# Query products from the third block of weights on in 16 bit parts

## What is computed

```python
def peer(h, peer_w_query, peer_keys1, peer_keys2, peer_u, peer_v):
    ...
    def block(xb):
        qh = (xb @ peer_w_query).reshape(-1, PEER_HEADS, 2, PEER_KEY_DIM // 2).astype(jnp.float32)
        s1 = jnp.einsum('thd,kd->thk', qh[:, :, 0], peer_keys1.astype(jnp.float32))
        s2 = jnp.einsum('thd,kd->thk', qh[:, :, 1], peer_keys2.astype(jnp.float32))
        v1, i1 = lax.top_k(s1, PEER_TOPK)
        v2, i2 = lax.top_k(s2, PEER_TOPK)
        ...
        act = jax.nn.gelu(jnp.einsum('thkd,td->thk', peer_u[e], xb).astype(jnp.float32))
        return jnp.einsum('thk,thkd->td', (g * act).astype(xb.dtype), peer_v[e])
```

## Time and profile before

| | us |
|---|---|
| median of three runs | 5007.54 |
| lowest and highest of the three | 4987.62, 5008.25 |
| profiled execution, device time | 5001.89 |
| its span in the trace | 5000.0 |
| TensorE busy with matmuls | 4677.6 (94% of the span) |
| VectorE busy | 2859.6 (57%) |
| ScalarE busy | 1316.0 (26%) |
| query phase on TensorE, first to last product | 2023.2 to 2292.4 |

### The profile page before, as it was taken

The page is one execution under the profiler, slowest core; times in us unless marked ns, Lnnn a source line. Parts: engine busy times, 40 slices in busy tenths (PEclk is TensorE's granted clock), DMA queues, the critical chain, the costliest instruction groups (busy, mean ns, idle before and its releaser), DMA issues. The chain is left out here.

```text
span 5000.0 us, 70223 instructions
## 1 busy us (share of the span) xinstructions
PE 4677.6 (94%) x26702; PEld 2940.9 (59%) x26702; DVE 2859.6 (57%) x5220; ACT 1316.0 (26%) x1829; POOL 782.6 (16%) x743
## 2 busy tenths in 40 slices
PE   5999989999778799899999999999997999999996
PEld 4666644555676465566666666666664555555553
DVE  3456414433355434314666766667543989889884
ACT  2223213332110000211444444444222222222221
POOL 0000100000000001000000000000002766666640
PEclk6999987876676899899999999999998999999998
DMA  4443532211233344223455555545445888888861
GB/s 152 163 160 122 175 103 64 69 56 54 83 107 105 136 170 176 75 68 130 169 194 191 180 190 184 205 176 189 168 155 211 311 301 294 292 297 300 293 231 72
DMA packets 367537, 846.13 MB, mean 169 GB/s; under 512 B 35986, under 2 KB 198418, under 8 KB 358482
## 3 DMA queue, kind: packets, MB, share of 16 engines
q1 hardware_dynamic: 251122, 472.45, 27.7%
q0 software_dynamic: 72352, 272.81, 15.7%
q10 hardware_dynamic: 43840, 97.93, 5.2%
HBM read 665.05 MB, written 178.03 MB: 169 GB/s over the span
## 5 line engine op out<-in xcount | busy, mean ns | idle before, releaser
L364 PE MATMUL dot_ps<-h_parts,u_parts 128*128 128x384 f16 (+1 forms) x9216 | 1452.9, 317 | 7.2 <-PEq L1846 4.5
L364 PEld LDWEIGHTS dot_ps<-h_parts,u_parts 128*128 128x128 f16 x9216 | 892.5, 98 | 498.3 <-issue 6.5
L364 PE MATMUL totals_ps<-act_parts,v_parts 128*128 128x416 f16 x6144 | 1083.8, 340 | 33.3 <-DVE act_parts L2728 33.2
L364 PEld LDWEIGHTS totals_ps<-act_parts,v_parts 128*128 128x128 f16 x6144 | 601.5, 98 | 514.3 <-issue 36.4
L377 PE MATMUL in_ps<-h_parts_in,in_parts 128*128 128x384 f16 (+1 forms) x3168 | 492.3, 318 | 5.3 <-DVE in_parts L693 4.5
L2443 DVE SCALAR_TENSOR_TENSOR u_parts<-u_chunks,units,u_parts 128x1024 f16<-128x1024 f32 x126 | 161.8, 1284 | 516.4 <-ACT u_parts L2227 516.4
L2236 ACT ACTIVATE gelu<-dot_ps,units 128x384 f32<-128x384 f32 (+1 forms) x384 | 215.9, 563 | 808.0 <-PE dot_ps L364 807.9
L377 PEld LDWEIGHTS in_ps<-h_parts_in,in_parts 128*128 128x128 f16 x3168 | 309.2, 98 | 182.5 <-DVE in_parts L693 4.6
L2795 POOL DMA_INDIRECT row_value<-tmp_g_rows,row_g x256 | 307.6, 1202 | 394.1 <-POOLq L2101 316.2
L2684 ACT ACTIVATE v_parts<-v_group,units 128x1024 f16<-128x1024 f32 x128 | 136.6, 1137 | 768.0 <-PE totals_ps L364 712.9
L2739 DVE SCALAR_TENSOR_TENSOR h<-totals_ps,sum_unit,h 128x416 f32<-128x416 f32 x388 | 247.6, 647 | 140.7 <-PE totals_ps L364 137.2
(11 more groups left out here) (340 smaller groups left out, 5598.8 us busy)
## 6 DMA issues: line engine op xcount, KB each, us to landing
u_chunks<-in_u SPq DMA_DIRECT2D x128, 512.0 KB, 5.6
v_sweep<-in_v SPq DMA_DIRECT2D x128, 512.0 KB, 4.7
v_group<-in_v SPq DMA_DIRECT2D x32, 2048.0 KB
tmp_g<-gelu ACTq DMA_DIRECT2D x128, 416.0 KB, 2.7
tmp_w<-h POOLq DMA_DIRECT2D x26, 2048.0 KB, 8.4
w_groups<-tmp_w SPq DMA_DIRECT2D x32, 1664.0 KB
gelu_in<-tmp_g SPq DMA_DIRECT2D x32, 1664.0 KB
merge_sweep<-in_u POOLq DMA_DIRECT2D x64, 512.0 KB, 5.5
```

The lines of the kernel that those rows point to most:

```text
L364: mm = pe.matmul(bank, left(x), right(y), start=first and x == 0 and y == 0, stop=last and x == 1)
```

## The change

Three things change.

1. From block 2 on (`WIDE = 2`) queries(c) is done in 16 bit parts, with `triple`: 72 float16 products in place of 24 float32 ones. For this each block of `w_query` is split too, into `wq16`, two buffers: the leading part by ScalarE (`lead_part`), the rest by VectorE (`rest_part`). Blocks 0 and 1 stay in float32.
2. The tokens' parts `h16` are made at once, all eight chunks behind `scales.ready` and ahead of queries(2), which now waits for them. For this `spread_out` moves up behind the first third of queries(1). The parts of the first two chunks of `u` move behind the takes of blocks 2 and 3.
3. The scale of `w_query` needs its largest value. The merge sweeps its sixteen blocks too: five sweeps in place of four to an output chunk, 80 in place of 64, with a ring of five buffers. Two further operations write `W_SCALE` and `Q_UNIT`, and one further reduction takes the largest of the sixteen.

At the start of the phase the loads of `wq` are now issued ahead of the load of the keys.

```diff
-        sweep = Sweep(nc, ctx, sem, "merge", a, s, SWEPT, NK - SWEPT, 4, [])
+        EACH = 5
+        sweep = Sweep(nc, ctx, sem, "merge", a, s, SWEPT, NK - SWEPT, EACH, [], 2 * EACH, range(2 * EH))
...
-                        for k in range(4):
-                            sweep.vector(dve, i, 4 * u + k)
+                        for k in range(EACH):
+                            sweep.vector(dve, i, EACH * u + k)
...
             def _(sp):
-                sp.dma_start(keys[:, :, :], a["keys"]).then_inc(keys_in, 16)
                 for c in range(RQ):
                     sp.dma_start(wq[:, c, :, :], a["w_query"][c]).then_inc(wq_in[c], 16)
+                sp.dma_start(keys[:, :, :], a["keys"]).then_inc(keys_in, 16)
...
-                        sp.wait_ge(q_done, (c + 1) * NS)
+                        if c < WIDE:
+                            sp.wait_ge(q_done, (c + 1) * NS)
+                        else:
+                            sp.wait_ge(wq_split, c - WIDE + 1)
...
-                def queries(c):
-                    pe.wait_ge(wq_in[c % RQ], 16 * (c // RQ + 1))
+                def queries(c, beside=None):
+                    if c < WIDE:
+                        pe.wait_ge(wq_in[c], 16)
+                    else:
+                        pe.wait_ge(h_split, KC)
+                        pe.wait_ge(wq_split, c - WIDE + 1)
...
+                            else:
+                                mm = triple(pe, q_ps[:, at % 4, 0:n], lambda x: wq16[:, c % 2, x, k, :],
+                                            lambda y: h16[:, y, k, t0:t0 + n], k == 0, k == KC - 1)
                         mm.then_inc(q_done, 1)
+                        if beside and q == 0:
+                            beside()
...
-                queries(1)
-                scales.spread_out(pe, 0)
+                queries(1, lambda: scales.spread_out(pe, 0))
...
+                def lead_part(c):
+
+                    act.wait_ge(wq_in[c % RQ], 16 * (c // RQ + 1))
+                    if c >= WIDE + 2:
+                        act.wait_ge(q_done, (c - 1) * NS)
+                    act.activation(wq16[:, c % 2, 0, :, :], wq[:, c % RQ, :, :], ACT.Copy,
+                                   scale=units[:, W_SCALE:W_SCALE + 1]).then_inc(wq_hi, 1)
...
-                for c in range(3):
+                take(0)
+                act.wait_ge(scales.ready, 1)
+                for k in range(KC):
+                    act.activation(h16[:, 0, k, :], h[:, k, :], ACT.Copy, scale=h_unit[:, 1:2]).then_inc(h_hi, 1)
+                lead_part(WIDE)
+                take(1)
+                lead_part(WIDE + 1)
+                for c in range(WIDE, K2):
                     take(c)
...
+                    if c + 2 < K2:
+                        lead_part(c + 2)
...
+                def rest_part(c):
+                    dve.wait_ge(wq_hi, c - WIDE + 1)
+                    dve.scalar_tensor_tensor(wq16[:, c % 2, 1, :, :], wq[:, c % RQ, :, :],
+                                             units[:, W_SCALE:W_SCALE + 1], wq16[:, c % 2, 0, :, :], ALU.mult,
+                                             ALU.subtract).then_inc(wq_split, 1)
+
+                for k in range(KC):
+                    dve.wait_ge(h_hi, k + 1)
+                    dve.scalar_tensor_tensor(h16[:, 1, k, :], h[:, k, :], h_unit[:, 1:2], h16[:, 0, k, :],
+                                             ALU.mult, ALU.subtract).then_inc(h_split, 1)
+                rest_part(WIDE)
+                take(0)
+                rest_part(WIDE + 1)
+                for c in range(1, K2):
...
+                    if WIDE + 2 <= c + 3 < K2:
+                        rest_part(c + 3)
```

More of the change, by code:

```diff
@@ L170, in build @@
             gain=keep("gain", [P, KC, 1 + NSEQ]),
-            u_tops=keep("u_tops", [P, NK]),
+            u_tops=keep("u_tops", [P, NK + 2 * EH]),
             units=keep("units", [P, 8]),
@@ L280, with __init__ @@
     STEP = 8
-    def __init__(self, nc, ctx, sem, name, a, s, first, count, ring, spare):
+    def __init__(self, nc, ctx, sem, name, a, s, first, count, ring, spare, step=STEP, also=()):
         self.a, self.s, self.first, self.count, self.ring = a, s, first, count, ring
+        self.step, self.also = step, also
         fresh = ring - len(spare)
-        own = ctx.enter_context(nc.sbuf_tensor(name + "_sweep", [P, fresh, KC * P], F32))
+        own = ctx.enter_context(nc.sbuf_tensor(name + "_sweep", [P, fresh, KC * P], F32)) if fresh else None
         self.buf = spare + [own[:, r, :] for r in range(fresh)]
@@ L1810, in _ @@
                                   spare[:, u, :, :]).then_inc(mix_taken, 1)
-                        for k in range(4):
-                            sweep.vector(dve, i + KC // 2, 4 * u + k)
+                        for k in range(EACH):
+                            sweep.vector(dve, i + KC // 2, EACH * u + k)
                 norm.vector(dve)
@@ L1824, in sb @@
             return ctx.enter_context(nc.sbuf_tensor(name, shape, dt))
-        K2, NT, RQ = 2 * EH, TILES + 1, 4
+        K2, NT, RQ, WIDE = 2 * EH, TILES + 1, 4, 2
         keys = sb("keys", [P, 2, NK])
         wq = sb("wq", [P, RQ, KC, P])
+        wq16 = sb("wq_parts", [P, 2, 2, KC, P], F16)
         qh = sb("qh", [P, 2, TP])
@@ L1909, in take @@
                         act.wait_ge(q_done, at + 1)
+                        unit = units[:, Q_UNIT:Q_UNIT + 1] if c >= WIDE else 1.0
                         if q == NS - 1:
-                            act.copy(qh[:, c % 2, T:TP], q_ps[:, at % 4, SEQ - t0:n]).then_inc(twice, 1)
-                        act.copy(qh[:, c % 2, t0:t0 + n], q_ps[:, at % 4, 0:n]).then_inc(q_taken, 1)
-                act.sem_inc(q_taken, 4)
-                for c in range(3):
-                    take(c)
-                act.wait_ge(scales.ready, 1)
@@ L1918, in _ @@
-                for c in range(2):
-                    act.wait_ge(s["u_in"][c], 16)
-                    act.activation(u16[:, 0, c, :, :], u[:, c, :, :], ACT.Copy,
-                                   scale=units[:, U_SCALE:U_SCALE + 1]).then_inc(s["u_hi"], 1)
-                for c in range(3, K2):
-                    if c < 3 + KC:
-                        k = c - 3
-                        act.activation(h16[:, 0, k, :], h[:, k, :], ACT.Copy,
-                                       scale=h_unit[:, 1:2]).then_inc(h_hi, 1)
-                    take(c)
+                            act.activation(qh[:, c % 2, T:TP], q_ps[:, at % 4, SEQ - t0:n], ACT.Copy,
+                                           scale=unit).then_inc(twice, 1)
```

51 lines of the change are left out of this document (28 added, 23 removed).

## The result

The changed kernel is faster: 4964.31 us in the median of six runs against 4997.2 in six of the kernel before. The ratio is 0.9916 with a 95% interval from 0.9892 to 0.9939, that is 42 us less, with 30 to 54 inside the interval; it is not the ratio of the two medians, which lie 33 us apart. One run of the changed kernel took 12098.69 us, more than twice any other; it is left out of the ratio, and its cause is open. The forecast was 46.6 us less, 4958 us.

The account below looks back on a forecast made before the run. The prediction took TensorE to bound the merge and query phase. It summed −48.6 (16 bit products) + 2.4 (wait) − 0.4 (load order) = −46.6 us, giving 4958 us, range 4938 to 4980.

Parts of the forecast that it names:

- Bound by TensorE: Merge and query phase: TensorE is the bound, busy 158.22 of 160 and 180.00 of 180 us; other engines have room.
- The 16 bit products: Query blocks from 2 on: 14.63 to 11.16 us each, 3.47 less, over fourteen blocks 48.6 us less.
- The wait ahead of queries(2): Before queries(2): TensorE stalls 2.4 us for the chain from spread_out through VectorE's eight rests and block 2's rest.
- The clock after the stall: Behind the wait before queries(2): a possible half-speed loss of 1.6 us, left out of the sum.
- the rival: Behind the wait before queries(2): the clock falls, one loss of 1.6 us, total 4960 us; chance 0.28.
- Splits, sweeps, loads: Query phase and merge: splits and sixteen further sweeps stay hidden, adding nothing; issuing the wq load first saves 0.4 us.
- All phases behind the queries as long as before: Dots phase and later: a sign of the forecast, no change in their lengths.
- a rival in which the gain is given back later: Dots phase start: set by something other than TensorE, such as the last scores' store; about 5000 us, chance 0.04.
- The level of 4958 us: Whole kernel: 4958 us, chosen with sums of 4955.3 from the profiled execution and 4960.9 from the runs' median.

Follow-up runs that it names:

- e2: Changed kernel with spread_out moved back behind queries(1): query phase 238.1 us against 226.1, ratio to the kernel before 0.9933.
- e4: Changed kernel with block 2's weights split before the tokens and queries(2) waiting chunk by chunk: query phase 223.5 us, ratio to before 0.9879.
- e7: Changed kernel executed once more without an edit, for its trace: query phase 226.7 us, dots phase 1561.9 us.
- e9: Changed kernel plus 20 unused float32 products (40 matmul instructions) ahead of the merge's branch loop: dots phase 1552.2 us, ratio to before 0.9909.
- e5: Changed kernel with every sweep of the merge done twice: merge 389.7 us, query phase 227.6 us, ratio to before 0.9924.
- e1: Kernel before with only the change's sixteen further sweeps and five buffers, queries left float32: merge 390.6 us, ratio to before 0.9989.
- e3: Changed kernel with 16 bit parts only from block 8 on: query phase 245.0 us, dots phase 1555.0 us, ratio to before 0.9962.
- e8: Kernel before executed once more without an edit, for its trace: query phase 273.4 us, dots phase 1551.8 us.
- e12: Kernel before plus 20 unused float32 products (40 matmul instructions) in the merge: query phase 273.3 us, dots phase 1551.9 us.

## Why the prediction was right, and where it was not

**Bound by TensorE.** Right. Both stages stayed without a gap, and a faster block moved the end by just what it saved.

**The 16 bit products.** Right, and a little short: 3.57 us a block instead of 3.47, 50.0 us in all. I took 11.16 us from the earlier trace rows, where the small matmul of the spread, which ends the stretch, starts 0.1 us late. Behind it in the same trace 216 such matmuls in one piece start at 208.39 and are followed at 241.58, which is 11.06 us for 72.

**The wait ahead of queries(2).** Right: 2.44 us against 2.4, by the steps that were named. The late spread (e2) and the waits by chunk (e4) show that this chain sets it.

**The clock after the stall.** The loss was left out of the sum, and in the trace of after it did not come: 19 matmuls ran in the first 3.0 us, at clock 1.00. That was in part luck. Of the four traces with this wait of 2.28 us, three (after, e7, e9) kept the clock, and e5 lost 1.68 us behind it. Behind 11.74 us (e2) the clock was at 0.50. So the reason given, that 2.4 us is nearer to the short gap, does not decide it: the rival happens in some executions.

**Splits, sweeps, loads.** Right: no wait in the steady state, a merge as long as before in e1 and with twice the sweeps in e5. The first product starts 0.48 us earlier behind its idle time (27.85 instead of 28.33 us; 0.4 was forecast). The other traces agree: 28.4 to 29.2 us with the keys first, 27.9 to 28.1 with the weights first. That the merge came out at 391.4 us both times in spite of it is chance: its first products lost 1.8 us more to the clock after the change, and those of the norm 1.7 us less.

The query phase is thus accounted for: −49.98 us for the blocks, +2.44 for the wait, −0.46 because the clock rose earlier in queries(0) (17.00 to 16.54 us), +0.35 in the idle time ahead of the dots phase (4.49 to 4.84 us), together −47.65, and −47.64 is measured. That idle time stands in this row:

```profile
2251.65 68.61 PE L365 MATMUL dot_ps<-h_parts,u_parts 128*128 128x384 f16 x426 [4.84 <-PEq L1850]
```

**All phases behind the queries as long as before.** This step failed. The dots phase took 8.4 us more, and 7.8 to 9.7 more in the two traces of the kernel as against its twin with 40 further matmuls (e9: 1552.2). I had a rival in which the gain is given back later, but for another reason, a start of the dots phase that does not follow TensorE, and with all of the gain. What came in its place is the changed length of TensorE's program: the second idle time at each jump, 5.5 us in the trace of after, and the lower clock behind one of them; the transfers of instructions (last section) show what TensorE waits for there. By the stages the gain is 47.6 less 8.4, that is 39 us. The whole came out at 42 and not at 47, which fits, but an interval of 30 to 54 can't tell 39 from 47.

**The level of 4958 us.** It was hit within 7 us, and that is in part luck. It was taken between two sums, and the higher of them rests on 5007.54 us, the median of three runs of before; the median of six is 4997.2. Less 46.6 that would be 4950.6, and 4964.31 is 13.7 above it.

## What to carry to other kernels

Where one engine is busy without a gap, price an edit by the start-to-start time of a like group of its instructions, and write the chain of new inputs out step by step: both came within 0.1 us here. A wait of some 2 us ahead of such a stretch has a price of its own, for the clock may fall behind it (once in four traces here, 1.7 us). Before adding a whole-operand wait, ask whether the consumer can start with the first chunk: the order (weights first) and a wait for each chunk took the 2.4 us away together. And when a change alters how much straight-line code stands ahead of a loop, look at the loop's jumps in the new trace: a border in the instruction stream close behind a jump cost 8 us in a phase that the change did not touch, and a few empty matmuls in an idle time moved it away.

## What the hardware showed unexpectedly

**A border in TensorE's instruction stream.** Its place follows the count of matmuls ahead of the loop with a period of 128: it is seen at three counts (80, 192 and 336 more), and at the four others (0, 40, 312 and 376 more) it is absent, as the theory has it. Behind a jump back TensorE idles there for 0.5 to 3.4 us, and the timeline names nothing that releases it; the trace of after has no other idle time of this kind in the dots phase.

The DMA view of after has a queue for instructions, q8, and it shows what TensorE waits for. Its row for the whole execution, and then for 2688.70 to 2690.00 us:

```profile
q8 instruction: 140, 2.29, 0.2%
```

```profile
q8 instruction: 1, 0.02, 4.2%
```

A transfer of q8 has 16384 bytes. In the query phase one starts every 124 to 127 matmuls on average, in float32 (about every 32 us) and in 16 bit parts (about every 19 us), so they follow TensorE's instructions. At the first jump of after one transfer starts at 2681.34 us, lands at 2682.29, and TensorE restarts at 2683.93. The next one starts at 2688.75, when the 28 matmuls are just done (2688.65), lands at 2689.63, and TensorE goes on at 2691.26. Between 2684.00 and 2688.70 the view has no row of q8.

All 28 jumps of the fourteen traces are alike in this: one transfer lands 1.6 to 1.8 us ahead of the restart, and the next starts 4.5 to 5.9 us behind the restart and takes 0.9 to 1.4 us, in the kernel before too (4.98 us at its first jump), where no border is near. In the fourteen jumps with a second idle time, TensorE goes on 1.3 to 1.7 us after this second transfer has landed, so 7.3 to 8.1 us behind the restart. In that time it can run some 45 to 50 matmuls at 163 ns (44 of them took 7.32 us in e3). So a border behind 28 costs some 3 us, one behind 44 less than one, and one behind 52 or more next to nothing. What holds the second transfer back for some 5 us is not shown.

The Trainium skill, page "Runtime: NRT & Kernel Launch", section "Instruction fetch mechanics", says that instructions are fetched in blocks of 256, one ahead of the other, and that a taken branch to a target outside the blocks at hand has to wait for a fetch. 128 matmuls with their weight loads are 256 instructions, and the trace agrees. The page puts the wait at the jump itself; here a second one comes at the next border.

**The same idle time, two clocks.** At the end of the merge TensorE idles 3.5 us ahead of the norm's products. In the kernel before, this was followed by a clock of 0.51. After the change the row is

```profile
1982.81 14.89 PE L231 MATMUL merge_ps<-y,const 128*128 128x384 f32 x48 [3.50 <-ACT y L220]
```

and the windows behind it, and behind the wait ahead of queries(2), are

```profile
1982.80:1986.80 4.00, 3.99 (x13) 2.58 (x14) 4.00 (x5) 4.00 (x5) 0.00 (x0) 1.00 0.98 418
...
2061.63:2064.63 3.00, 3.00 (x19) 1.83 (x20) 2.49 (x4) 0.00 (x0) 0.00 (x0) 1.00 0.23 70
```

The clock stayed at 1.00 (2.4 GHz) behind 3.50 us, where it had fallen to 1.2 GHz behind 3.49. The group took 14.89 us instead of 16.59. So an idle time of this length may or may not cost 1.7 us, from one execution to the next. The difference is no effect of an edit: of the fourteen traces, all with 3.49 or 3.50 us there, in five the group took 16.59 us (before, e7, e8, e9, e12) and in nine 14.89, and both kernels are on both sides. At 2.28 us the clock fell in one of four (e5). The Trainium skill says as much, page "TensorE: Matmul & The Clock Gate", section "What's actually happening": the window over which activity is judged runs on its own.
